# Triangular inverse kept in a PSUM bank and copied out by ScalarE; modulation chunks 0 to 4 loaded and summed later; output gate in halves

## The reference, cut to what matters

```python
# layer 1, delta rule, for 4 heads and 4 chunks of 64 tokens
a_strict = where(strict, (k_beta @ k.T) * l_mask, 0)
t_mat = a_strict + eye(64)
value      = triangular_solve(t_mat, v_beta, lower, unit_diagonal)
k_cumdecay = triangular_solve(t_mat, k_beta * exp(decay), ...)
# then a scan over the 4 chunks; its output is gated by silu(dgate)

# layer 2, modulation: 6144 sums over 1024 rows of w_ada
mod = silu(c) @ w_ada + b_ada
sh1, sc1, g1, sh2, sc2, g2 = split(mod, 6)
h = rmsnorm(x) * (1 + sc1) + sh1          # first used here
...
x = x + g1 * (merged @ w_out)             # used near the end of layer 2
h2 = rmsnorm(x) * (1 + sc2) + sh2         # used after that
```

## Time and profile before

| | us |
|---|---|
| median of 3 runs | 1138.16 |
| lowest and highest run | 1137.22 and 1146.73 |
| profiled execution, its own time | 1137.32 |
| its span, first to last instruction | 1135.5 |
| TensorE busy in it | 1106.6 |
| VectorE, ScalarE, GpSimd busy | 603.9, 501.5, 151.2 |

### The profile page before, as it was taken

How to read it: one execution, slowest core, us unless ns; L and a number is a source line. 1 busy time by engine, 2 the same in 40 slices (tenths; PEclk the granted TensorE clock), 3 DMA queues, 4 the chain that set the end, 5 groups by cost and what they waited for, 6 DMA issues and landing times.

```text
span 1135.5 us, 18601 instructions
## 1 busy us (share of the span) xinstructions
PE 1106.6 (97%) x7625; PEld 843.2 (74%) x7625; DVE 603.9 (53%) x925; ACT 501.5 (44%) x827; POOL 151.2 (13%) x111
## 2 busy tenths in 40 slices
PE   8999799999999999999999999999999999999996
PEld 7987678999878888778888876666666666666663
DVE  5988676879956784785755652222222222222223
ACT  6665654654433746645556252222222222222223
POOL 1339960422000040400000000000000000000000
PEclk9999999999999999999999999999999999999999
DMA  9862825477486756644548579999999999999994
GB/s 314 280 215 77 297 93 201 161 263 257 183 306 204 243 176 223 211 162 154 174 157 329 209 288 423 421 426 423 423 425 420 425 422 421 425 424 421 426 421 175
DMA packets 82701, 332.05 MB, mean 292 GB/s; under 512 B 4555, under 2 KB 6926, under 8 KB 66110
## 3 DMA queue, kind: packets, MB, share of 16 engines
q1 hardware_dynamic: 81236, 328.43, 74.6%
q0 software_dynamic: 1088, 2.34, 1.0%
q10 hardware_dynamic: 298, 0.11, 0.1%
HBM read 329.83 MB, written 1.05 MB: 291 GB/s over the span
## 4 chain that ended last, share of the span: by engine, by line
PE 80%; DVE 8%; DMA 7%; issue 2%; ACT 2%; SPq 1%; DVEq 0%; ACTq 0%
PE bank L1113 18%; PE bank L451 12%; PE bank L453 12%; PE bank L452 12%; PE bank L1132 9%; PE bank L1103 5%; DMA ring<-in_w_exp_down 3%; DVE ring_r L1844 2%; DMA ring<-in_w_in 2%; DVE arena L1924 2%; PE bank L1160 1%; PE bank L1161 1%; DMA ring<-in_w_ff 1%; DMA ring<-in_w_ada 1%; PE bank L1120 1%
## 5 line engine op out<-in xcount | busy, mean ns | idle before, releaser
L1844 DVE TENSOR_TENSOR ring_r<-ring,arena_r 128x2048 fp32r<-128x2048 f32 x93 | 217.9, 2355 | 118.5 <-ACT arena_r L1333 116.9
L1333 ACT ACTIVATE arena_r<-ring 128x2048 fp32r<-128x2048 f32 x93 | 177.4, 1918 | 170.1 <-PE bank L453 71.7
L453 PE MATMUL bank<-arena_r,actT_r 128*128 128x512 f32 x384 | 150.5, 392 | 0.0
L451 PE MATMUL bank<-arena_r,tok_r 128*128 128x512 f32 x352 | 140.8, 400 | 1.7 <-DVE con L2331 1.7
L452 PE MATMUL bank<-ring_r,tok_r 128*128 128x512 f32 x352 | 138.2, 393 | 0.0
L2688 POOL TENSOR_TENSOR ring<-ring 128x512 f32<-128x512 f32 x63 | 102.5, 1652 | 253.7 <-ACT ring L1424 251.9
L2503 DVE TENSOR_TENSOR arena<-bank,arena 64x512 f32<-64x512 f32 x62 | 42.7, 688 | 175.3 <-PE bank L1132 174.6
L451 PE MATMUL bank<-tok_r,arena_r 128*128 128x256 f32 x352 | 99.5, 283 | 1.8 <-DVE actT_r L1861 1.2
L453 PE MATMUL bank<-tok_r,ring_r 128*128 128x256 f32 x352 | 98.3, 279 | 0.0
L452 PE MATMUL bank<-actT_r,arena_r 128*128 128x256 f32 x352 | 98.2, 279 | 0.0
L2489 DVE TENSOR_TENSOR arena<-bank,arena 128x256 f32<-128x256 f32 x32 | 13.6, 425 | 151.3 <-ACT arena L1763 93.9
(11 more groups left out here) (424 smaller groups left out, 1770.7 us busy)
## 6 DMA issues: line engine op xcount, KB each, us to landing
ring<-in_w_in SPq DMA_DIRECT2D x22, 2048.0 KB, 9.6
ring<-in_w_exp_down SPq DMA_DIRECT2D x22, 2048.0 KB, 21.3
ring<-in_w_exp_gate SPq DMA_DIRECT2D x21, 2048.0 KB, 21.9
arena<-in_w_exp_up SPq DMA_DIRECT2D x21, 2048.0 KB, 23.5
ring<-in_w_ff SPq DMA_DIRECT2D x16, 2048.0 KB, 7.8
ring<-in_w_ada SPq DMA_DIRECT2D x12, 2048.0 KB, 10.9
arena<-in_w_exp_gate SPq DMA_DIRECT2D x11, 2048.0 KB, 21.5
arena<-in_w_exp_down SPq DMA_DIRECT2D x10, 2048.0 KB, 21.4
```

Source lines behind the costliest of these rows:

```text
L451: mm(o, l[0], r[0], start=start, stop=False)
L453: return mm(o, l[1], r[0], start=False, stop=stop)
L1333: A(hi, w, ACT.Copy).then_inc(S["w_high"], 1)
L1844: TT(half(i, ringR)[0], w, hi.bitcast(fp32), ALU.subtract).then_inc(S["w_rest"], 1)
```

## The change

- **Levels.** `DI` and `DT` become one 512-wide tile per t, `DIT[t]`: inverse on the left, turned copy on the right. Level 0 makes both by products into one bank for each t. That bank is held (`held`) over all five levels: each level's corrections are added to what is in it, without a new start, and ScalarE copies all of it out (`inverse_copies`, 512 wide, 256 wide for the last). VectorE's `corrected` is gone. The other jobs take turns in the remaining six banks.
- **Gate.** The product `dg` is made in two halves, one in level 0 and one in level 1.
- **Modulation.** Chunks 0 to 4 leave the levels and the recurrence. Chunk 0 is turned behind the last `out_product`, 1 and 2 take the places of 5 and 6 in the first feed-forward matrix, 3 comes into the second, where 7, 8 and 9 move as well, and 6, 4 and 5 go behind steps 4, 10 and 14 of layer 2. VectorE now sums 0, 3, 7, 8, 9, 6, 4 and 5; ScalarE and GpSimd share 1, 2, 10 and 11. The total of loads is the same.
- The order of VectorE's and ScalarE's lists in the levels is written anew, with the exponentials between the copies, and the two banks of `kc` are filled in turns.

```diff
-        ET, DI, DT, YY, AT, MT = [x[:, 0:8 * C] for x in (ar(15360, 1024), DQ, DK, QD, kbT, qT)]
+        ET, YY, AT, MT = [x[:, 0:8 * C] for x in (ar(15360, 1024), QD, kbT, qT)]
+        DIT = [x[:, 0:8 * C] for x in (DQ, DK)]
...
-        ADA_BY_POOL = (0, 4)
-        ADA_BY_DVE = (7, 8, 9)
-        DVE_MOD = {4: 8, 10: 9}
-        ADA_FF1 = {2: 5, 5: 6}
-        ADA_FF2 = {1: 7, 3: 8, 6: 9}
-        ADA_STEP = {3: 10, 6: 11}
+        ADA_BY_POOL = (1, 2, 10, 11)
+        ADA_BY_DVE = (0, 3, 7, 8, 9, 6, 4, 5)
+        DVE_FF2 = {3: 7, 5: 8, 10: 9}
+        DVE_STEP = {3: 6, 9: 4, 13: 5}
+        ADA_FF1 = {2: 1, 5: 2}
+        ADA_FF2 = {1: 3, 3: 7, 4: 8, 6: 9}
+        ADA_STEP = {3: 10, 4: 6, 6: 11, 10: 4, 14: 5}
...
-        ADA_BEHIND = {("win", 2): (0,), ("win", 6): (1, 2, 3, 4), ("ff1", 2): (5,), ("ff1", 5): (6,), ("ff2", 0): (7,),
-                      ("ff2", 3): (8,), ("ff2", 6): (9,), ("win2", 2): (10,), ("win2", 6): (11,)}
+        ADA_BEHIND = {("wout", 1): (0,), ("ff1", 2): (1,), ("ff1", 5): (2,), ("ff2", 0): (3,), ("ff2", 3): (7,),
+                      ("ff2", 4): (8,), ("ff2", 6): (9,), ("win2", 2): (10,), ("win2", 4): (6,), ("win2", 6): (11,),
+                      ("win2", 9): (4,), ("win2", 13): (5,)}
...
         def job(name):
+            while turns[0] % 8 in held:
+                turns[0] += 1
             turns[0] += 1
...
                 for t in range(T):
                     wait_read(pe, f"Y{l}{t}")
-                    if l:
-                        wait_read(pe, f"Dt{l - 1}{t}")
-                    if not last:
-                        product(f"Dn{l}", DT, YY, t)
-                    product(f"Dt{l}", YY, DT, t)
+                    bk = begin_at(f"D{l + 1}{t}", held[t])
+                    for turned in (1,) if last else (0, 1):
+                        for h in range(DH):
+                            for r in (0, C):
+                                two = (turned_inverse(4 * t + h, r), within(YY)(4 * t + h, r))
+                                i = mm(bk[r:r + C, (4 * turned + h) * C:(4 * turned + h + 1) * C], two[turned],
+                                       two[1 - turned], start=False, stop=True, skip_group_check=True)
+                    end(i, f"D{l + 1}{t}")
...
             out_product(1, 1, lambda: turn_x1(0))
+            ada(0)
...
+            def inverse_copies(l, ts=range(T)):
+                for t in ts:
+                    bk = wait_full(act, f"D{l}{t}")
+                    o = slice(256 if l == len(LEVELS) else 0, 256 if l == 0 else 512)
+                    done(copy(DIT[t][:, o], bk[:, o]), f"D{l}{t}")
...
             o_rest(1)
-            mod_cols(4)
-            for c in range(4):
-                wait_read(dve, f"mod{c}")
-            step(STT(sc1, modc[:, 8:16], 1.0, col("nmix", 0, 8), ALU.add, ALU.mult))
+            mod_sums(0)
             add_x(1, 0, 0)
             add_x(2, 1, 0)
...
-            mod_sums(7)
+            mod_sums(3)
             for i in range(F1 + 16 + NH, W2 + 2):
                 w_rest(i)
                 x = i - NH - F1 - 16
                 if x % 2 and x // 2 in ADA_FF2:
                     mod_cols(ADA_FF2[x // 2])
-                if x in DVE_MOD:
-                    mod_sums(DVE_MOD[x])
+                if x in DVE_FF2:
+                    mod_sums(DVE_FF2[x])
```

More of the change, by code:

```diff
@@ L440, in ada @@
                 else:
-                    by_pool = [x for x in range(c + 1) if x not in ADA_BY_DVE]
-                    pe.wait_ge(S["pool_step"], 1 + 3 * len(by_pool) + sum(x <= c for x in ADA_BY_POOL))
+                    pe.wait_ge(S["pool_step"], 4 + 3 * ADA_BY_POOL.index(c))
                 w = weights("ada", c)
@@ L664, in att_values, with dg_half @@
                 end(i, f"ao{t}")
+            def dg_half(h):
+                w = wait_split("win", 6, h)
+                for t in range(T):
+                    if h == 0:
+                        dg.append(begin(f"dg{t}"))
+                    i = part(dg[t], (aH, aL), t, h, w)
+                    if h == 1:
+                        end(i, f"dg{t}")
+                if h == 0:
+                    i.then_inc(S["half_used"], 1)
+                else:
+                    last_job[place[("win", 6)]] = "dg1"
+            dg = []
             def fill(l):
-                if l == 0:
-                    split_product("win", 6, "dg")
-                elif l == 1:
-                    ada(0)
+                if l < 2:
+                    dg_half(l)
                 elif l == 2:
-                    ada(1)
                     att_turn()
@@ L682, in _ @@
                 for t in range(T):
[L683 to L684 removed]
+                    wait_read(pe, f"D{l}{t}")
+                    chunk_products(f"Y{l}", t, lambda bk, h, r: bk[r:r + C, h * C:(h + 1) * C], within(AT), inverse)
                     if t == 0:
@@ L2157, in _, with mod_sums @@
             o_rest(1)
-            mod_cols(4)
-            for c in range(4):
-                wait_read(dve, f"mod{c}")
-            step(STT(sc1, modc[:, 8:16], 1.0, col("nmix", 0, 8), ALU.add, ALU.mult))
+            def mod_sums(c):
+                n = place[("ada", c)]
+                dve.wait_ge(w_in[n % NR], 16 * (n // NR + 1))
+                w = weights("ada", c)
+                step(TS(w[:, 0, :], w[:, 0, :], cs[:, 0:1], None, ALU.mult))
+                for k in range(1, KT):
+                    i = STT(w[:, 0, :], w[:, k, :], cs[:, k:k + 1], w[:, 0, :], ALU.mult, ALU.add)
+                    if k < KT - 1:
+                        step(i)
+                i.then_inc(S["mod_summed"], 1)
+            mod_sums(0)
             def add_x(n, c, t):
@@ L2231, in _ @@
                     mod_cols(ADA_FF2[x // 2])
-                if x in DVE_MOD:
-                    mod_sums(DVE_MOD[x])
+                if x in DVE_FF2:
+                    mod_sums(DVE_FF2[x])
+            for c in range(4):
+                wait_read(dve, f"mod{c}")
+            step(STT(sc1, modc[:, 8:16], 1.0, col("nmix", 0, 8), ALU.add, ALU.mult))
             def add_ff(j):
@@ L2700, in _ @@
             pool.dma_start(rowsB[:, 0:16], g["const"][:, o + P:o + P + 16]).then_inc(S["fold_in"], 16)
-            for c in range(5, 12):
-                if c not in ADA_BY_DVE:
-                    ada(c)
+            for c in ADA_BY_POOL:
+                ada(c)
             wait_full(pool, "rout1")
```

169 lines of the change are left out of this document (74 added, 95 removed).

## The result

The changed kernel takes 1154.97 us (median of 4 runs, 1153.32 to 1155.23). The kernel before, run beside it, took 1138.37 (1137.22 to 1146.73). The ratio is 1.0128, its 95% interval 1.0087 to 1.0170: slower by 1.3%, and clearly slower, though the interval reaches a little under 1%. 1154.97 lies within the range on record. The profiled execution took 1155.09, its span is 1153.2: 17.77 us more than the profiled one of before.

A forecast was written before the change was run, and what follows sets the result against it. TensorE, busy 1106.6 of 1135.5 us, was taken to bound the kernel. Its terms, from -5.2 for the levels to +12.3 for layer 2's step 3, summed to +19.3 on the profiled 1137.32; median forecast 1157 us, range 1146 to 1163.

The forecast's parts named there:

- levels: Delta levels, 100 to 150 us: 8.05 us of TensorE gaps close, 1.15 of products and 1.7 of gaps added: -5.2.
- five turns moved: Modulation chunks 0 to 4 leave levels and recurrence and come back later, 0.66 us each on both sides: 0.
- chunk 0 ahead of the additions, its columns: Before the transposes of x, TensorE waits +1.7 us for VectorE's sum; the columns, ahead of a ff1 half, +0.2.
- second feed-forward matrix: Turning of chunk 8 waits 6.4 us behind late ff2 chunk 5; an old 1.08 us wait goes: +5.3.
- layer 2, step 3: `kv` waits for ScalarE's copies, which stand behind the late load of chunk 5 of `w_in_2`: +12.3 us.
- chunk 4 at steps 9 and 10: Layer 2: chunk 11 of `w_in_2` loads later, so VectorE's sum of chunk 4 comes late for TensorE: +2.2 us.
- clock: TensorE's granted clock falls behind the two long waits: 1.89 us for `kv`, half at the shorter wait: +2.8.
- The two gaps that should stay: In the levels: 0.75 us for a gate tile's bank in level 2, 0.85 behind exponentials in level 4.
- the likeliest rival: At layer 2, step 3, ScalarE meets its load in time and `kv` doesn't wait: 1143, within 1%; chance 0.14.
- The levels got shorter: Judges the rival that the levels don't get shorter, ScalarE's copies queueing: term +1.2, 1163 us; chance 0.10.
- The clock rival: The clock stays low longer: 4.6 us more, 1162 us; chance 0.06.
- the forecast of over 1%: Whole kernel slower by over 1%, above 1149.5 us; chance 0.80.

The follow-up runs named there:

- m_mods: The kernel before with the changed placing and summing of the modulation chunks alone, levels, gate and banks as before: 1155.97 us, ratio 1.0092 to the kernel before.
- e2_cols: The changed kernel with the columns of modulation chunk 7 taken right behind the sums of chunk 8: 1151.04 us, ratio 1.0048 to the kernel before.
- e1_six: The changed kernel with modulation chunk 6 one place further back, behind chunk 5 of `w_in_2`: 1150.78 us, ratio 1.0045 to the kernel before.
- the later groups: Experiment groups, each with the kernel before run beside it; there it took 1145.41, 1145.05, 1144.72 and 1145.37 us.
- e4_four: The changed kernel with modulation chunk 4 summed at step 10 and turned behind step 11: 1155.08 us, ratio 1.0089 to the kernel before.
- e6_addx: The changed kernel with the sums of modulation chunk 0 behind the first two additions to x: 1153.22 us, ratio 1.0098 to the kernel before.
- the execution of 1145.53: The kernel before, unchanged, run again for a profile of a long execution: 1145.53 us, one run.
- that of 1137.11: The kernel before, unchanged, run once more for a profile: 1137.11 us, one run.
- e5_kc: The changed kernel with the products of `kc` one bank after the other again: 1155.82 us, ratio 1.0084 to the kernel before.
- b1_all: The changed kernel with chunk 6 later, chunk 7's columns earlier, chunk 4 at step 11, chunk 0's sums behind the additions: 1147.01 us, ratio 1.0024.

## Why the prediction was right, by its own steps

| step | forecast | measured |
|---|---|---|
| levels | -5.2 | -6.5 |
| five turns moved | 0 | -0.3 |
| chunk 0 ahead of the additions, its columns | +1.7, +0.2 | +1.5, 0 |
| second feed-forward matrix | +5.3 | +2.7 |
| start of layer 2 | none | +1.1 |
| layer 2, step 3 | +12.3 | +10.6 |
| the retention heads' transposes, step 7 | none | +0.8 |
| chunk 4 at steps 9 and 10 | +2.2 | +2.2 |
| clock | +2.8 | +5.1 |
| sum | +19.3 | +17.2, of 17.8 in all |

*Levels.* 91.2 us became 83.7; with 1.5 of the new wait and 2.5 for the five turns that left, -6.5. The two gaps that should stay did, 0.84 at the copies behind two heads of exponentials and 0.63 (forecast 0.85 and 0.75). What was missed is `kc` in turns: 1.0 us for two tiles. The cause was only half right: the working gave the gain to the additions and scalings taken out. `m_mods` shows that most of it came with the modulation's leaving, scalings among it, and about 1.4 us with the new levels and gate halves (2.0 less the 0.6 of `kc`). The working's sentence that ScalarE's and GpSimd's work on these chunks lay beside TensorE's doesn't hold: it made over half of the gaps.

*Second feed-forward matrix.* The mechanism is shown by `e2_cols`. The size was off by the landing: the load of ff2 chunk 5 was in 8.1 us after its issue (323.2 to 331.3), not 10.9.

*Step 3.* The mechanism is shown by `e1_six`. The landing took 9.3 us (426.50 to 435.77), not 10.9: that is nearly the whole difference.

*Chunk 4.* The load of chunk 11 of `w_in_2` was issued at 510.35, ScalarE had it at 519.33, 9.0 us later where 8.7 was taken, and ropes, half and sum followed as in the working.

*Two waits unseen.* At the start of layer 2 TensorE was 2.4 us ahead of its time before, but the first half of `w_in_2` only 0.9: its load took 10.0 us from its issue to ScalarE (351.84 to 361.79), against 8.4 before. VectorE, which then takes the columns of chunk 9, came 1.1 us late to the additions. At step 7 ScalarE came to the two halves 12.6 us later than before (480.00 against 467.43) and TensorE to its transposes 11.8 later; ScalarE had stood 3.05 us for the load of chunk 11, which is let go later now. Both are landings on lists that the working had passed over as unchanged.

*Clock.* Three falls of 1.7 us each, 5.1 in all, where the sum had 1.9 for one and half of it for another. The third came behind 2.21 us, a wait of a length for which no price was made. These two errors, landings too slow and clock too cheap, are of opposite sign (4.3 and 2.3 us); that the sum came out better than its terms is luck.

*The rivals.* `kv` waited, so the likeliest rival fell. The levels got shorter. The clock rival (4.6 more) was nearer than its 0.06 said: half of it came. What no step held is that the kernel before itself has executions of 1145 to 1152 us. Against the medians of 1145 in the later groups, the change costs some 10 us and not 17. `e4_four`, with the same median as the changed kernel, has a ratio of 1.0089 there. So the forecast of over 1% is borne out beside the four runs of the result, and would have been close to the line beside the later ones.

## What to carry to other kernels

When a chunk is put into a ring, write down for every place how many products ahead its load is let go. In the changed kernel two extra places within one turn of the ring took a product's length off that lead, and both long waits stood there. Then ask what stands behind the late load in each list: moving one instruction (`mod_cols`) took 3.8 us down to 0.5 with the load as late as before. Work that is moved away from one full engine has to be priced in each list it goes to: four of these moves, undone singly, gave back 4 us, 4 us, nothing and 2 us. Before a scattered time is put down to chance, compare a short and a long execution of the same kernel instruction by instruction: here a 0.87 us delay stood at the head of 6.8 lost ones, and a first fall of the clock had shifted VectorE into that delay.

## What the runs showed of the hardware

- In the recurrence, a stretch of short products, the granted clock of TensorE fell 2 to 3 us behind waits of 0.59 and 0.74 us and then stayed at 1.2 GHz for 13.6 us, although TensorE was counted busy throughout (2.00 of 2.00 us in each stretch). In the twelve other profiles this wait is missing and the clock didn't fall there. That the wait is the cause is likely and not proven: two profiles have both, and in `e6_addx` a fall came with no wait ahead of it.
- The same wait doesn't always have a fall behind it. The 2.84 us ahead of the last level had one in the execution of 1145.53 and none in that of 1137.11; the wait of 2.2 us for chunk 4 had one in the changed kernel, and none in the same place of the version with `kc` undone (2.17) or of `e6_addx` (2.18). All 19 waits of 3.25 us or more in the profiles have one.
- Outside the recurrence a fall cost between 1.4 us (`e5_kc`, ahead of chunk 8's turning) and 3.0 us (`e6_addx`, the same place). In the changed kernel it was 1.7 each time.
- A two-input VectorE instruction of 0.69 us took 1.40 and 1.56 beside GpSimd's additions, and 0.69 with GpSimd idle, or where it began 0.1 us or less before the end of one. In a row of seven, each took 0.75 us alone and 1.63 to 1.67 beside them (`e1_six`, `b1_all`).
